# Weight lows of the first network's first projections: a negating ScalarE pass and an adding GpSimd DMA in place of a VectorE subtraction

## The reference, cut to what matters

```python
def swiglu(h, w_in, w_out):
    a, b = jnp.split(h @ w_in, 2, axis=-1)
    return (jax.nn.silu(a) * b) @ w_out

def trunk_layer(x, mod, n_pre, n_post, f_in, f_out, mix_w, ctx):
    sh0, sc0, g0, sh1, sc1, g1, sh2, sc2, g2 = jnp.split(mod, N_MOD, axis=-1)
    h = rms_norm(x, n_pre[0]) * (1 + sc0) + sh0
    x = x + 0.5 * g0 * rms_norm(swiglu(h, f_in[0], f_out[0]), n_post[0])
    ...
```

## Time and profile before

| | |
|---|---|
| median of 2 runs | 1796.2 us (1794.91 and 1797.48) |
| span of the profiled execution, first to last instruction | 1796.0 us |
| mean granted clock of TensorE | 0.991 |
| TensorE busy | 1746.6 us (97%) |
| VectorE, ScalarE, GpSimd busy | 1106.0, 726.5, 52.8 us |
| DMA | 183.82 MB, mean 102 GB/s |

### The profile page before, as it was taken

How to read it: one execution, slowest core, us unless ns; L and a number is a source line. 1 busy time by engine, 2 the same in 40 slices (tenths; PEclk the granted TensorE clock), 3 DMA queues, 4 the chain that set the end, 5 groups by cost and what they waited for, 6 DMA issues and landing times.

```text
span 1796.0 us, 30974 instructions
## 1 busy us (share of the span) xinstructions
PE 1746.6 (97%) x12362; PEld 1671.4 (93%) x12362; DVE 1106.0 (62%) x1968; ACT 726.5 (40%) x1310; POOL 52.8 (3%) x45
## 2 busy tenths in 40 slices
PE   6999999999999999999999999989999999999998
PEld 4999999999988999999999888889979999999997
DVE  4866566766457434555537877774458835973974
ACT  4432222212355312343454555553654433541554
POOL 0000000000020000000000000000113000000001
PEclk8999999999999999999999999999999999999999
DMA  8444444433213224323243211112412222232231
GB/s 352 140 155 141 146 138 154 147 134 118 77 42 141 71 71 94 92 87 96 78 141 117 70 39 40 39 40 71 153 62 91 72 90 72 74 107 59 92 133 59
DMA packets 53022, 183.82 MB, mean 102 GB/s; under 512 B 8593, under 2 KB 11299, under 8 KB 51875
## 3 DMA queue, kind: packets, MB, share of 16 engines
q1 hardware_dynamic: 52899, 182.10, 30.9%
HBM read 164.90 MB, written 16.52 MB: 101 GB/s over the span
## 4 chain that ended last, share of the span: by engine, by line
PE 90%; DVE 5%; ACT 2%; issue 1%; DMA 1%; SPq 0%; DVEq 0%; ACTq 0%
PE psum L649 18%; PE psum L650 17%; PE psum L651 17%; PE psum L632 4%; PE psum L633 4%; PE psum L634 4%; PE psum L689 2%; PE psum L691 2%; PE psum L690 2%; PE psum L1128 2%; PE psum L1118 2%; PE psum L1093 2%; PE psum L1008 1%; DMA mw<-in_w_mod 1%; PE psum L1176 1%
## 5 line engine op out<-in xcount | busy, mean ns | idle before, releaser
L649 PE MATMUL psum<-h_hi,whi 128*128 128x320 f32 x1520 | 478.7, 315 | 3.5 <-ACT sa L1459 3.3
L651 PE MATMUL psum<-h_hi,wlo 128*128 128x320 f32 x1520 | 470.9, 310 | 0.0
L650 PE MATMUL psum<-h_lo,whi 128*128 128x320 f32 x1520 | 470.7, 310 | 0.0
L1813 DVE TENSOR_TENSOR wlo<-raw,whi 128x1024 fp32r<-128x1024 f32 (+1 forms) x155 | 193.3, 1247 | 382.9 <-ACT whi L1223 382.9
L649 PEld LDWEIGHTS psum<-h_hi,whi 128*128 128x128 f32 x1520 | 286.1, 188 | 9.7 <-issue 5.5
L650 PEld LDWEIGHTS psum<-h_lo,whi 128*128 128x128 f32 x1520 | 286.3, 188 | 1.0
L651 PEld LDWEIGHTS psum<-h_hi,wlo 128*128 128x128 f32 x1520 | 286.1, 188 | 0.0
L1223 ACT CAST whi<-raw 128x1024 fp32r<-128x1024 f32 (+1 forms) x155 | 161.1, 1041 | 207.0 <-PE psum L651 189.8
L649 PE MATMUL psum<-g_hi,whi 128*128 128x320 f32 x512 | 158.4, 309 | 0.0
L650 PE MATMUL psum<-g_lo,whi 128*128 128x320 f32 x512 | 158.4, 309 | 0.0
L651 PE MATMUL psum<-g_hi,wlo 128*128 128x320 f32 x512 | 158.4, 309 | 0.0
(11 more groups left out here) (415 smaller groups left out, 3680.9 us busy)
## 6 DMA issues: line engine op xcount, KB each, us to landing
raw<-in_w_ffn_in SPq DMA_DIRECT2D x88, 512.0 KB, 3.6
raw<-in_w_mix SPq DMA_DIRECT2D x77, 512.0 KB, 4.1
mw<-in_w_mod SPq DMA_DIRECT2D x28, 768.0 KB, 4.9
raw<-in_w_ffn_out SPq DMA_DIRECT2D x32, 512.0 KB, 3.5
mw<-in_w_mod SPq DMA_DIRECT2D x4, 2048.0 KB, 18.1
gate<-gate_keep SPq DMA_DIRECT2D x24, 320.0 KB, 4.5
mw<-in_w_mod SPq DMA_DIRECT2D x14, 512.0 KB, 4.2
gate_keep<-gate SPq DMA_DIRECT2D x20, 320.0 KB, 4.8
```

Of the source, the lines that this page charges most:

```text
L649: mm(out, whi[t.slot][:, k, :], hi[:, k, cols], start=(k == 0), stop=False)
L650: mm(out, whi[t.slot][:, k, :], lo[:, k, cols], start=False, stop=False)
L651: last = mm(out, wlo[t.slot][:, k, :], hi[:, k, cols], start=False, stop=(k == nk - 1))
L1813: tt(lo[:, 0:nk, :], raw[t.raw][:, 0:nk, :], hi[:, 0:nk, :].bitcast(F32), ALU.subtract).then_inc(raw_free, 1)
```

## The change

In the input rounds of the first network, the low part is made in another way. ScalarE, behind the high part, writes `-raw` rounded to fp32r, that is the negated high part, into `wlo`. GpSimd then issues a DMA that adds `raw` onto `wlo` in place (`accum_op`), waits for its completion, waits until `raw_free` has the count of the tile before, and raises it by one. VectorE does no split there. This holds for 43 tiles: those two ahead of every input tile, 16, 16 and 11, the last of the third phase left out. The splits of all other tiles stay on VectorE, with one added wait for `raw_free`, so that the count rises in the order of the tiles. Three places of the diff, with new functions whole:

```diff
+            def split_and_negate(t):
+                act.wait_ge(raw_in[t.raw], 16 * (t.quad + 1))
+                act.wait_ge(tile_done, t.n + 1)
+                copy(whi[t.slot][:, :, :], raw[t.raw][:, :, :])
+                fn(wlo[t.slot][:, :, :], raw[t.raw][:, :, :], ACT.Copy, scale=-1.0).then_inc(w_hi, 1)
...
+                            elif f == 0:
+                                split_and_negate(t.plus(2))
                             elif not peeled:
                                 split(t.plus(2))
...
+            def low_of(t, n):
+                pool.wait_ge(w_hi, t.n + 1)
+                pool.dma_start(wlo[t.slot][:, :, :].bitcast(F32).rearrange("p k c -> p (k c)"),
+                               raw[t.raw][:, :, :].rearrange("p k c -> p (k c)"), accum_op=ALU.add).then_inc(low_in, 16)
+                pool.wait_ge(low_in, 16 * (n + 1))
+                pool.wait_ge(raw_free, t.n + RAWS)
+                pool.sem_inc(raw_free, 1)
+
+            base = lows = 0
+            for p, nj in enumerate(PHASES):
+                for u in range(2 * nj - (p == 2)):
+                    low_of(Tile(base + 2 + u), u + lows)
+                lows += 2 * nj
+                base += 2 * nj + KC
...
             def split(t, to=None, nk=KC):
                 hi, lo = to or (whi[t.slot], wlo[t.slot])
                 dve.wait_ge(w_hi, t.n + 1)
+                dve.wait_ge(raw_free, t.n + RAWS)
                 tt(lo[:, 0:nk, :], raw[t.raw][:, 0:nk, :], hi[:, 0:nk, :].bitcast(F32), ALU.subtract).then_inc(raw_free, 1)
...
-                            elif not peeled:
+                            elif f and not peeled:
                                 split(t.plus(2))
```

More of the change, by code:

```diff
@@ L364, in build @@
         dve_sums, tok_sum, tok_hi, tok_lo = mod0_in
-        mod0_mm, mod0_copy, mod0_ev, ld_cst = sem("mod0_mm"), sem("mod0_copy"), sem("mod0_ev"), sem("ld_cst")
+        mod0_mm, mod0_copy, low_in, ld_cst = sem("mod0_mm"), sem("mod0_copy"), sem("low_in"), sem("ld_cst")
         cols_in = sem("cols_in")
```

## The result

The changed kernel takes 1847.45 us in the median of two runs (1843.26 and 1851.64), the kernel before 1796.2. The ratio is 1.0286, with a 95% interval of 1.0263 to 1.0309. The forecast was 1852. The profiled execution of the changed kernel took 1851.6 us, with a span of 1849.7: 53.7 us over the span of before.

What follows compares the result with a forecast made beforehand. TensorE was taken as the only bound in the first network's input projections. Its waits for low parts, 52.8 us over 11 rounds plus 1.8 and 0.9, gave 55.5; 1796.0 + 55.5 = 1851.5, rounded to 1852 us, range 1807 to 1920.

Steps and rivals of the forecast that it cites:

- VectorE's 53 us: In the first network's input projections, VectorE loses 43 splits of 1.225 us, none on the path, so worth 0.
- D: Time from ScalarE's signal through GpSimd's issue, adding transfer and waits to the rise of `raw_free`; put at 7.0 us.
- slacks of 4 to 6 us: Time left from ScalarE's signal to TensorE's start: 4.2, 4.8, 5.0 and 5.7 us behind u=0 to u=3.
- the 4.2 us behind u = 0: Slack from ScalarE's pass ending at 86.3 to TensorE's first matmul of tile u=2 at 90.44.
- The 5.0 us behind u = 2: Slack from ScalarE's end at 100.4, with silu starting earlier at 97.7, to TensorE's start at 105.44.
- the sum without sharing: Low-part path without company: 3.6 us plain load, 1.2 second read, 0.4 dearer issue and signals.
- The sharing: Weight and modulation loads issued when `raw_free` rises fly beside the next adding transfer; priced at 1.8 us.
- only u=0 and u=2 cost: TensorE waits only before even tiles, 2.8 and 2.0 us, 4.8 us per round, 52.8 over 11 rounds.
- the opposite case: A TensorE wait before an even tile delays the next odd tile's deadline too, so odd tiles cost nothing.
- three signs that I had named for a wrong prediction: Landing below 5 us, TensorE's clock falling in the stretch, or waits appearing before odd tiles.
- my third rival: TensorE's clock falls after its waits in the stretch, 37 to 81 us on top, 50 taken: 1902 us; chance 0.15.
- the transfer fits: Second read and sharing cost little, the low-part path takes 3.6 to 6.1 us, 1797 to 1832 us; chance 0.27.

Runs made afterwards that it cites:

- even-only kernel: Against the changed kernel, only even-numbered tiles get the new low part and VectorE splits the odd ones as before; 1814.78 us, ratio 1.011.
- odd tiles alone: Against the changed kernel, only odd-numbered tiles get the new low part and VectorE splits the even ones as before; 1800.05 us, ratio 1.0027.
- the kernel with the held-back loads: Against the kernel with new low parts for odd tiles only, SyncE holds modulation loads until ScalarE's signal for the next odd tile; 1866.52 us, ratio 1.0388.
- half by DMA: Against the changed kernel, GpSimd's DMA adds and ScalarE negates only half of each low part, VectorE subtracts the other; 1801.79 us, ratio 1.0027.

## Why the prediction was right, and where it was not

**The frame held.** TensorE had nothing to win, VectorE's 53 us were worth 0, and what decided was D against slacks of 4 to 6 us. The even-only kernel bears out the 4.2 us behind u = 0. ScalarE's pass ends there at 85.65, and the last matmul of the tile before starts at 89.75, so the next could start at 89.90. The path took 4.9 us to TensorE's start at 90.56, so TensorE lost 0.7, of which the list shows 0.5. The 5.0 us behind u = 2 that kernel does not test. VectorE splits the odd tiles in it, so `macc_hi` stands in front of the silu again, at 97.74, and the slack there was 4.4.

**D was right in size: 7.0 forecast, 6.8 at the median** (0.3 from ScalarE's end to the issue, landing 6.4, under 0.1 to the rise). Its parts were roughly right too. Alone it is 4.7, where the sum without sharing had 5.2. The sharing is 2.0 at the median, where I had 1.8. But the sharing is no constant: from 0 to 5.7 us, by what flies beside.

**The step that failed: "only u=0 and u=2 cost".** It assumed one D for all tiles. Here are the 43 transfers by the place in the round that they stand behind, with TensorE's listed waits for them, counted from the timelines of the changed kernel:

| behind | transfers | landing, median us | waits for them | forecast |
|---|---|---|---|---|
| u = 0 | 11 | 4.4 | 4, 3.7 us | 11, 32.6 us |
| u = 1 | 11 | 6.4 | 10, 14.4 us | none |
| u = 2 | 11 | 7.7 | 7, 8.9 us | 11, 22.9 us |
| u = 3 | 10 | 7.2 | 7, 8.9 us | none |

Two thirds of the waiting, 23.3 of 35.9 us in 17 of 28 waits, stand before odd tiles, which the forecast had at nothing (2.31 us at 126.85 is one). The place priced highest, u = 0, cost next to nothing: SyncE issues at most a weight load around its transfer, and no modulation load. The long transfers are those issued just after `raw_free` rose for the tile before, with the weight load and a modulation load right around them. A late transfer raises `raw_free` late, moves those loads under the next transfer and so makes that one long. And TensorE's wait before an odd tile gives the next even one that much more time, just as the forecast said of the opposite case.

With odd tiles alone the loads are released by VectorE, some 6 us before the transfer (SyncE at 98.51 and 99.18, GpSimd at 104.59), and TensorE waits only once. The kernel with the held-back loads shows the same cause from the other side.

**The sum came out by luck, through errors that offset.** Forecast were 55.5 us of waits, all before even tiles, with the clock kept. Measured are 33.5 us of waits after the first tile (35.9 less 2.4), most of them before odd tiles, while the stage is 51.3 longer. Two of the three signs that I had named for a wrong prediction came: waits before odd tiles, and a clock that fell. So the nearness of 1852 to 1847 says nothing for the mechanism. The clock was my third rival, and it came in part. These eight windows of 10 us hold all of its falls (clock third from the end):

```profile
60.00:70.00 10.00, 7.64 (x42) 7.62 (x42) 6.91 (x11) 3.78 (x4) 0.86 (x1) 0.83 0.83 193
70.00:80.00 10.00, 8.15 (x45) 7.89 (x44) 0.00 (x0) 2.59 (x3) 0.86 (x1) 0.83 0.69 174
260.00:270.00 10.00, 8.04 (x51) 7.78 (x50) 4.77 (x7) 4.96 (x6) 1.46 (x2) 0.92 0.79 193
270.00:280.00 10.00, 10.00 (x61) 9.24 (x59) 0.82 (x1) 2.63 (x3) 0.67 (x2) 0.91 0.75 188
300.00:310.00 10.00, 8.16 (x45) 7.90 (x45) 1.29 (x2) 2.92 (x4) 0.86 (x1) 0.83 0.73 189
340.00:350.00 10.00, 8.18 (x44) 7.38 (x43) 5.18 (x10) 2.62 (x3) 0.86 (x1) 0.85 0.68 166
350.00:360.00 10.00, 9.91 (x66) 9.65 (x66) 4.24 (x7) 2.60 (x3) 0.86 (x1) 0.98 0.67 158
470.00:480.00 10.00, 7.58 (x41) 7.38 (x41) 8.12 (x16) 2.00 (x3) 0.90 (x1) 0.83 0.66 143
```

The shares missing to 1.00 add up to 1.02, so 10.2 us of full speed. I had priced this rival at 37 to 81, with a fall at each wait; there were six falls. (The upper end was also read too high: from 26 to 36 us the clock of the kernel before was 0.80, then 0.50 for 6 us, then 0.99, which is 6.8 us of the low level and not 7.5.)

That leaves 7.6 us (51.3 - 33.5 - 10.2), and the waits account for nearly all of it. The list counts a wait from the end of the last matmul, which is shown 0.31 us long, while the next could have started 0.147 after its start: 0.16 us more. And the matmul behind the first one comes 0.25 us after it (126.85 and below) and not 0.147: 0.10 us more.

```profile
127.10 0.31 PE L650 MATMUL psum<-h_lo,whi 128*128 128x320 f32 x1
```

For the 27 waits after the first that is an estimate of 7 us. The even-only kernel agrees, at an unchanged clock: its stage (60.72 to 495.92) is 13.3 us longer than before, with 8.1 us of listed waits in it, which leaves 5.2 over 17 waits, 0.3 each.

**The rival "the transfer fits"** would have held for a plain copy: 2.8 us alone from GpSimd, 1800 us. By the Trainium skill ("DMA: Bandwidth & Descriptors", section "Anatomy of one DMA") an estimate of 3.2 us for 512 KB is near that, and the trace agrees for a copy (3.1 at the median). For an adding transfer it is 1.2 us too short when alone, and 3.2 at the median of the changed kernel. That page also states ("Issuing engines are not separate DMA queues") that transfers run on the same 16 DMA engines, whichever engine issues them. The two landings of the copy, 3.1 us from either queue, are in keeping with it.

**No version beat the kernel before.** The nearest that compute the same, odd tiles only and half by DMA, are 0.3% slower. The stage has no idle TensorE time to give back.

## What to carry to other kernels

Compare the time left until the waiting engine's deadline with the time of the new path, not busy shares: moving 53 us off an engine with 144 us idle bought nothing, and a path of 4.7 to 10.9 us in place of 1.2 cost 51. Before putting a DMA into a chain that repeats with every tile, look at what its own completion sets off on other queues, and whether that will fly beside the next one. And when an engine is freed, see who had been hidden by it: the margin of 1.3 us on `macc_lo` was in no list of waits.

## What the hardware showed that I had not expected

- A DMA that adds, 512 KB within SBUF, took 4.4 us alone against 2.8 for a copy. Its median rose by 2.0 us in company and the copy's by 0.3, but that does not show that adding is more sensitive. The copy ends sooner, so in its kernel most modulation loads are issued 2 us and more before the next copy, and in the changed kernel most of them later than that. Where both had the same 512 and 768 KB about equally close in front, both suffered alike. Here is an adding transfer of the changed kernel, then a copy, each behind SyncE's two loads: 3.1 and 3.4 us more than alone.

```profile
108.17 0.33 SPq L429 DMA_DIRECT2D raw<-in_w_ffn_in  x1
108.79 0.33 SPq L436 DMA_DIRECT2D mw<-in_w_mod  x1
109.57 0.86 POOL L1797 DMA_DIRECT2D wlo<-raw  x1 [6.97 <-ACT wlo L1229]
DMA to landing us min/median/max: 7.5/7.5/7.5
```
```profile
60.81 0.33 SPq L429 DMA_DIRECT2D raw<-in_w_ffn_in  x1
61.46 0.33 SPq L436 DMA_DIRECT2D mw<-in_w_mod  x1
62.27 0.53 POOL L1797 DMA_DIRECT2D wlo<-raw  x1 [3.99 <-ACT wlo L1229]
DMA to landing us min/median/max: 6.2/6.2/6.2
```

- Of the two issued together at 103.31 the modulation load was hardly slowed, with 5.2 us (4.9 before), while the adding transfer took 7.7 (4.4 alone). Whether a copy within SBUF would lose as much when issued together with a load was not tried.
- The clock did not follow the length of a wait alone. A wait of 1.83 us before 302.11 stands in a window at 0.83, but the wait of 2.31 us before 126.85 in one at 1.00:

```profile
120.00:130.00 10.00, 7.69 (x52) 7.43 (x52) 6.96 (x11) 2.60 (x3) 0.86 (x1) 1.00 0.68 170
```

- With waits of mostly 3 us and more (held-back loads) the stage ran at 0.95; with waits of 0.4 to 1.1 us after the first tile it stayed at 1.00.
